# Decoder step: four page numbers in one load, and all value transfers of the sample attention issued by SyncE

## The chip, the core and the metric

The kernel runs on one core of a Trainium2 chip. A core has TensorE (PE in the profile), VectorE (DVE), ScalarE (ACT), GpSimd (POOL) and SyncE (SP), which only issues transfers and waits, and 16 DMA engines that move the data. SyncE and ScalarE each have a queue from which they issue transfers. The metric is the time of one execution in microseconds on the device.

## The reference

One layer of a hybrid decoder for a prompt of 512 rows and for 8 sample sequences of 8 new rows each (width 1024). The change concerns the attention of the samples. Each sequence b has two units, one for each mixer:

```python
# mixer A (m = 0): 8 heads x 64, window of 2048 cached keys, three dilated patterns
kk = jnp.concatenate([cache_win_k[b], k], 1);  vv = jnp.concatenate([cache_win_v[b], v], 1)
o = dilated_mix(q, kk, vv, L + jnp.arange(DS))
...
# mixer B (m = 1): 4 heads x 2 maps of 64, values of 128, over 16 pages of 128 rows
pk = ck[page_table].reshape(DB, P, N_HEADS_B, 2, HEAD_DIM)
pv = cv[page_table].reshape(DB, P, N_HEADS_B, 2 * HEAD_DIM)
a = softmax(q1 k1) - lam * softmax(q2 k2);  o = a @ v
```

Which pages belong to a sequence stands in `page_table` (8 x 16 whole numbers), an input. So the kernel has to read a page's number on the chip before it can issue the page's transfer. A page of keys or of values is 128 rows of 2 KB, 256 KB.

## The kernel before

**Stages.** Conditioning and input projection (to about 240 us), the prompt's attention (mixer A, to about 305), the sample attention together with the rest of the prompt's attention (mixer B), from about 310 to 655 us, then the output projection, the first norm, the gated ConvFFN and the second norm.

**Units and groups.** The list `sa` holds 16 units w = (m, b), mixers in turn. A unit's keys and values are cut in groups: m = 0 has three (two of 1 MB, one of 512 KB), m = 1 has four of four pages. Groups are numbered through, G = 0 to 55. Keys have 3 buffers (`kraw`), values 4 (`vg`).

**Work on a group.** VectorE transposes the keys (`turn_keys`, line 1145) and counts `kg_t`. TensorE scores them (`score_group`, line 1697). When all groups of a unit and its new rows are scored (`sa_s`), VectorE finds the minimum (lines 1243 to 1260), ScalarE takes exponentials (877 to 882), TensorE transposes them, and `weigh_group` (1729) multiplies with the values and counts `sa_vg`. The weighting of unit w's group g is placed behind the scoring of unit w+1's group g. Between these each unit also carries two units of the prompt's mixer B (`scores_b`, `turn_b`, `weigh_b`; ScalarE's `probs_b` at line 857 and `copy_b` at 866).

**Order on SyncE.** In one written-out order: for each G the keys of G, after `kg_t` says that buffer G-3 has been turned, then the values of group G-3 (`values_behind`, line 567), after `sa_vg` says that the buffer of four groups before is free; at the end of each unit from the third on the new rows of that unit (`load_new`, lines 425 and 426). Behind the last keys (G = 55) come the values of 52 to 55.

**Order on ScalarE.** `values_by_act` names the value groups that SyncE leaves out and ScalarE issues: of each unit but the first the groups 0 and 1 for m = 1, and group 1 for m = 0. They stand in ScalarE's order behind the copy at line 891, some ahead of `probs_b`, some behind (lines 892 to 898). ScalarE's activations behind them in its order wait for them to be issued.

**A page.** For a page of keys (lines 591 and 593) or values (446 and 448) the queue runs a load of the number from `pages` into a register (TENSOR_LOAD), a computation of bounds (FUSED_REGOPS), an assertion (SEQ_ASSERT), an address computation and the issue (DMA_DIRECT2D). Window loads have fixed addresses: keys 584 and 587, values 438 and 442.

Of the kernel before, what the change touches and what calls it, by code (L numbers as in the profile page):

```python
# [23 lines left out]
N_PAGES = PAST // PAGE  # L24
# [50 lines left out]
def build(nc, a, o, spill):  # L75
# [6 lines left out]
    with ctx:  # L82
        def sb(name, shape, dt=F32):
            return ctx.enter_context(nc.sbuf_tensor(name, shape, dt))
# [36 lines left out]
        pages = sb("pages", [1, DB * N_PAGES], I32)  # L121
# [250 lines left out]
        sa = [(m, b) for b in range(DB) for m in range(2)]  # L372
# [13 lines left out]
        for r, n in enumerate(rope_units):  # L386
            sec, t = units[n]
# [29 lines left out]

        def values_by_act(w, g):

            return w < len(sa) and w > 0 and (g < 2 if sa[w][0] else g == 1)  # L420

        def load_new(eng, w):

            m, b = sa[w]
            eng.dma_start(kn[0:DS, w % 2, :], k_s[DS * b:DS * b + DS, m, :]).then_inc(new_in[w % 2], 16)
            eng.dma_start(vn[0:DS, w % 2, :], v_s[DS * b:DS * b + DS, m, :]).then_inc(new_in[w % 2], 16)

        def load_values(eng, w, g):

            m, b = sa[w]  # L430
            win_v = flat_v[0][b].rearrange("(g r) h d -> g r (h d)", r=16)
            G = NG[w] + g
            vs = G % NV
            if G >= NV:
                eng.wait_ge(sa_vg, G - NV + 1)
            if m == 0 and g < 2:
                for t in range(4):
                    eng.dma_start(vg[vs][t:P:4, :, :],
                                  win_v[:, 4 * g + t, :].rearrange("(i m) f -> m i f", i=4)).then_inc(vg_in[vs], 16)
            elif m == 0:  # L440
                for t in range(2):
                    eng.dma_start(vg[vs][32 * t:32 * t + 32, :, :],
                                  win_v[96:128, 8 + 4 * t:12 + 4 * t, :]).then_inc(vg_in[vs], 32)
            else:
                for t in range(4):
                    pg = eng.value_load(pages[0:1, N_PAGES * b + 4 * g + t:N_PAGES * b + 4 * g + t + 1],
                                        min_val=0, max_val=a["cache_v"].shape[1] - 1)
                    eng.dma_start(vg[vs][t:P:4, :, :],  # L448
                                  flat_v[1][bass.ds(pg, 1)].rearrange("a (i m) h d -> m (a i) (h d)", i=4))\
                        .then_inc(vg_in[vs], 16)  # L450
# [3 lines left out]
        def _(sp):  # L454
# [105 lines left out]

            sp.wait_ge(page_in, 16)
            load_values(sp, 0, 0)
            load_values(sp, 0, 1)
            sp.wait_ge(w_used, CHUNK_AT[("ada", 9)] + 1)
            group_list = [(w, g) for w, (m, b) in enumerate(sa) for g in range(len(groups[m]))]

            def values_behind(G):

                if G >= 2 and not values_by_act(*group_list[G]):
                    if G == 2:  # L570
                        sp.wait_ge(pa_min, NU)
                    load_values(sp, *group_list[G])

            for w, (m, b) in enumerate(sa):
                win_k = flat_k[0][b].rearrange("(g r) h d -> g r (h d)", r=16)
                for g, nt in enumerate(groups[m]):
                    G = NG[w] + g
                    ks = G % NK
                    if G == 2:
                        sp.wait_ge(w_used, CHUNK_AT[("ada", 11)] + 1)  # L580
                    if G >= NK:
                        sp.wait_ge(kg_t, G - NK + 1)
                    if m == 0 and g < 2:
                        sp.dma_start(kraw[ks][:, :, :], win_k[:, 4 * g:4 * g + 4, :]).then_inc(kg_in[ks], 64)
                    elif m == 0:
                        for i in range(4):
                            sp.dma_start(kraw[ks][32 * i:32 * i + 32, 0:2, :],
                                         win_k[96:128, 8 + i:16:4, :]).then_inc(kg_in[ks], 16)
                    else:
                        for t in range(4):  # L590
                            pg = sp.value_load(pages[0:1, N_PAGES * b + 4 * g + t:N_PAGES * b + 4 * g + t + 1],  # L591
                                               min_val=0, max_val=a["cache_k"].shape[1] - 1)
                            sp.dma_start(kraw[ks][:, t, :], flat_k[1][bass.ds(pg, 1)].rearrange("a p h d -> (a p) (h d)"))\  # L593
                                .then_inc(kg_in[ks], 16)
                    if G >= 3:
                        values_behind(G - 3)
                if w >= 2:
                    sp.wait_ge(kn_t, w - 1)
                    sp.wait_ge(sa_pv, w - 1)
                    load_new(sp, w)  # L600
# [65 lines left out]
        def _(pool):  # L666
# [21 lines left out]
            for _, what, r in sorted(jobs):  # L688
                if what == "split":
                    n = CHUNK_AT[("in", r)]  # L690
                    for k in range(0, KT_D, 2):
                        if r == 0:
                            pool.wait_ge(in0_high, k // 2 + 1)
                        else:
                            pool.wait_ge(win_high, 4 * (r - 1) + k // 2 + 1)
                        w = slot(SLOT_OF[n])[:, k, :]
                        high, rest = pair_of(n, k)
                        nc.gpsimd.tensor_tensor(rest, w, high.bitcast(F32), ALU.subtract).then_inc(win_pool, 1)
                    if r == 0:
                        rest_of_ht(0)  # L700
                    continue
                s, t = units[rope_units[r]]
                sample_k = s in (1, 4) and t == TP
                pool.wait_ge(pj_d, r + 1)
                if not sample_k and r >= 4:
                    if (prev := last_t[r]) is not None:
                        pool.wait_ge(qk_t, prev)
                    if (q := last_store[r]) > 0:
                        pool.wait_ge(stg[r % 4], 16 * q)
                rows = P if t < TP else NS  # L710
                dst = k_s[:, s // 3, :] if sample_k else stage[0:rows, r % 4, :]
                nc.gpsimd.tensor_tensor(dst, tmp_a[0:rows, r % 2, :], tmp_b[0:rows, r % 2, :], ALU.add)\
                    .then_inc(rope_ok, 1)
# [56 lines left out]
        def _(act):  # L770
# [47 lines left out]
            for _, what, n in sorted(jobs):  # L818
                s, t = units[n]
                rows = P if t < TP else NS  # L820
                if what == "v":
                    act.wait_ge(pj_mm, n + 1)
                    dst = vp[:, t, s // 3, :] if t < TP else v_s[:, s // 3, :]
                    nc.scalar.activation(dst, bk(n % 4)[0:rows, :], ACT.Copy).then_inc(pj_a, 1)
                else:
                    k = tr_units.index(n)
                    act.wait_ge(qk_t, k + 1)
                    src = bk(4 + k % 2).rearrange("p (f t) -> p f t", f=4)
                    m0 = 8 * (s // 3)
                    for h in range(2):  # L830
                        last = nc.scalar.activation(qtp[64 * h:64 * h + 64, m0 + h:m0 + 8:2, P * t:P * t + P],
                                                    src[64 * h:64 * h + 64], ACT.Copy)
                    last.then_inc(qk_a, 1)
# [11 lines left out]
            act.wait_ge(out_sem, 16 * (TP * 2 + 2 * DB + 2))  # L845
            act.wait_ge(new_zero, 3)
            load_new(act, 0)
            load_new(act, 1)

            def probs_b(y):  # L850
# [17 lines left out]
            for w, (m, b) in enumerate(sa):  # L868
# [23 lines left out]
                if values_by_act(w + 1, 0):  # L892
                    load_values(act, w + 1, 0)
                probs_b(2 * w)
                if values_by_act(w + 1, 1):
                    load_values(act, w + 1, 1)
# [85 lines left out]
        def _(dve):  # L982
# [117 lines left out]
            jobs += [(5 * c - 1.4, "split", c) for c in range(1, 6)]  # L1100
            dve.wait_ge(rope_in, 16)
            for _, what, n in sorted(jobs):
                if what == "split":
                    for k in range(KT_D):
# [937 lines left out]
```

## Time and profile before

| what | value |
|---|---|
| median of 3 runs | 1250.76 us (1249.6 to 1254.75) |
| the profiled execution | 1249.29 us, its span 1247.3 us |
| PE busy | 1059.1 us, 85% of the span |
| DVE busy | 838.5 us, 67% |
| ACT busy | 269.2 us, 22% |
| POOL busy | 356.9 us, 29% |
| DMA | 276.55 MB, mean 222 GB/s |
| granted TensorE clock, mean | 0.911 |

A row of the stretches gives, for a stretch A:B in microseconds from the span's start, its length, then the busy time of PE, PEld (weight loads), DVE, ACT and POOL with the number of instructions in brackets, then the granted TensorE clock as a share, the DMA engines' busy share and GB/s. A row of the chain or of the timeline begins with its start and its length. Names with a q (SPq, ACTq) are the instructions of an engine's queue, issues of transfers above all. A merged row such as "x4" reaches from the start of its first instruction to the end of its last. A row on one line of the kernel gives the count and the least, median and greatest duration in nanoseconds.

### The profile page before, as it was taken

To read this page: it belongs to the slowest core of one execution; us is meant where nothing else is said; L and a number is where in the kernel's file an instruction comes from. 1 tells how busy PE (TensorE), PEld (TensorE's weight loads), DVE (VectorE), ACT (ScalarE), POOL (GpSimd) and SP (SyncE) were. 2 spreads that over 40 slices of the span, in tenths; PEclk is the share of its full clock that TensorE was granted. 3 is DMA by queue.
4 is the path that set the end of the run, shared out by engine and by line. 5 is a ranking of instruction groups with operands and counts; after the bars stand their busy time and mean duration, and the time that the engine had idled before them with its cause. 6 is when DMAs were issued, how large, how long until landed. Compare 5 with 4: busy or idle time off the path is not lost.

```text
span 1247.3 us, 24201 instructions
## 1 busy us (share of the span) xinstructions
PE 1059.1 (85%) x9389; PEld 856.2 (69%) x9389; DVE 838.5 (67%) x1521; ACT 269.2 (22%) x588; POOL 356.9 (29%) x378
## 2 busy tenths in 40 slices
PE   4599999999677677777776996999999999999994
PEld 2377777666455455555545774999999999777772
DVE  1657457267665767667749568367677676998968
ACT  0310010232222223222234103223222232100002
POOL 2333243100000000000007004356565565434323
PEclk8699999999787788779787897999999999999997
DMA  8948894686999999999991206177557731412202
GB/s 305 404 163 314 306 363 148 215 298 231 315 296 307 336 352 303 342 326 320 317 316 60 63 26 219 62 275 270 203 202 254 283 137 69 147 56 89 75 27 76
DMA packets 112551, 276.55 MB, mean 222 GB/s; under 512 B 9608, under 2 KB 33174, under 8 KB 108837
## 3 DMA queue, kind: packets, MB, share of 16 engines
q1 hardware_dynamic: 99125, 250.82, 59.2%
q10 hardware_dynamic: 13312, 24.19, 5.7%
q8 instruction: 75, 1.23, 0.4%
q14 instruction: 39, 0.32, 0.1%
HBM read 264.60 MB, written 76.69 MB: 274 GB/s over the span
## 4 chain that ended last, share of the span: by engine, by line
PE 58%; DVE 17%; SPq 10%; DMA 7%; issue 5%; POOL 2%; ACT 1%; ACTq 0%; DVEq 0%; POOLq 0%; PEldq 0%
PE wide L1572 16%; PE wide L1573 15%; PE wide L1574 15%; DVE ring L1145 3%; DMA ring<-in_cache_k 3%; SPq L591 3%; PE wide L1646 2%; SPq L593 2%; DMA ring<-in_w_ada 2%; PE wide L1635 2%; DVE ring_r L1077 2%; PE wide L1521 1%; SPq L448 1%; DMA ring<-in_w_down 1%; PE wide L1697 1%
## 5 line engine op out<-in xcount | busy, mean ns | idle before, releaser
L741 POOL TENSOR_TENSOR ring_r<-ring,ring_r 128x1024 fp32r<-128x1024 f32 x70 | 184.4, 2642 | 273.5 <-DVE ring_r L1037 204.5
L1572 PE MATMUL wide<-x_sb_r,ring_r 128*128 128x288 f32 x704 | 211.6, 301 | 8.2 <-DVE ht_r L1059 5.1
L1573 PE MATMUL wide<-ht_r,ring_r 128*128 128x288 f32 x704 | 209.4, 298 | 0.0
L1574 PE MATMUL wide<-x_sb_r,ring_r 128*128 128x288 f32 x704 | 208.6, 296 | 0.0
L1574 PE MATMUL wide<-ring_r,ht_r 128*128 128x512 f32 (+1 forms) x400 | 158.7, 397 | 0.0
L1145 DVE STREAM_TRANSPOSE ring<-ring 128x512 f32<-128x512 f32 x208 | 129.2, 674 | 34.7 <-DMA ring<-in_cache_k 34.7
L1572 PEld LDWEIGHTS wide<-x_sb_r,ring_r 128*128 128x128 f32 x704 | 133.4, 190 | 11.7 <-issue 11.2
L1574 PEld LDWEIGHTS wide<-x_sb_r,ring_r 128*128 128x128 f32 x704 | 134.2, 191 | 0.0
L1573 PEld LDWEIGHTS wide<-ht_r,ring_r 128*128 128x128 f32 x704 | 133.8, 190 | 0.0
L1697 PE MATMUL wide<-ring,x_sb 128*32 128x128 f32 (+1 forms) x1792 | 70.9, 309 | 49.5 <-DVE ring L1145 47.9
L1572 PE MATMUL wide<-ring_r,x_sb_r 128*128 128x512 f32 (+1 forms) x240 | 97.7, 407 | 11.0 <-DVE ht_r L1059 8.9
L1697 PEld LDWEIGHTS wide<-ring,x_sb 128*32 128x32 f32 x1792 | 54.5, 127 | 66.9 <-DVE ring L1145 57.5
L723 POOL COPY x_sb<-ring 32x128 f32<-32x128 f32 x64 | 18.4, 287 | 272.9 <-PE wide L1697 270.8
L1573 PE MATMUL wide<-ring_r,x_sb_r 128*128 128x512 f32 (+1 forms) x240 | 95.1, 396 | 0.0
L1572 PE MATMUL wide<-ring_r,ht_r 128*128 128x512 f32 (+1 forms) x220 | 88.2, 401 | 4.3 <-DVE ht_r L1397 2.4
L1574 PEld LDWEIGHTS wide<-ring_r,ht_r 128*128 128x128 f32 (+1 forms) x400 | 72.6, 181 | 21.5
L1573 PE MATMUL wide<-ring_r,ht_r 128*128 128x512 f32 (+1 forms) x220 | 86.7, 394 | 0.0
L1411 DVE SCALAR_TENSOR_TENSOR room<-room,vec_t 128x512 f32<-128x512 f32 x44 | 59.9, 1361 | 39.7 <-ACT room L954 39.6
L946 ACT ACTIVATE room<-wide,vec_t 128x576 f32<-128x576 f32 x44 | 32.7, 744 | 206.2 <-PE wide L1574 201.5
L1413 DVE SCALAR_TENSOR_TENSOR room<-room,vec_t 128x512 f32<-128x512 f32 x44 | 69.5, 1579 | 1.6
L1646 PE MATMUL wide<-room 128*128 128x128 f32 x320 | 58.3, 320 | 11.0 <-ACT room L866 9.8
L1037 DVE CAST ring_r<-ring 128x1024 fp32r<-128x1024 f32 x62 | 41.9, 687 | 36.1 <-DMA ring<-in_w_up 29.7
(225 smaller groups left out, 1894.0 us busy)
## 6 DMA issues: line engine op xcount, KB each, us to landing
ring<-in_cache_k SPq DMA_DIRECT2D x128, 256.0 KB
out_wks<-in_cache_win_k SPq DMA_DIRECT2D x8, 4080.0 KB, 19.0
out_wvs<-in_cache_win_v SPq DMA_DIRECT2D x8, 4080.0 KB, 24.7
ring<-in_w_ada SPq DMA_DIRECT2D x12, 2048.0 KB, 10.2
ring<-in_w_up SPq DMA_DIRECT2D x22, 1024.0 KB, 7.3
ring<-in_cache_win_k SPq DMA_DIRECT2D x16, 1024.0 KB
ring<-in_w_in SPq DMA_DIRECT2D x6, 2048.0 KB, 18.5
room<-in_cache_v ACTq DMA_DIRECT2D x32, 256.0 KB
```

The source lines that it names most:

```text
L591: pg = sp.value_load(pages[0:1, N_PAGES * b + 4 * g + t:N_PAGES * b + 4 * g + t + 1], min_val=0, max_val=a["cache_k"].shape[1] - 1)
L741: nc.gpsimd.tensor_tensor(rest, w, high.bitcast(F32), ALU.subtract).then_inc(wl_rest, 1)
L946: nc.scalar.activation(u_b[:, k % 2, 2:2 + NT].rearrange("p (h t) -> p h t", h=2), pair, ACT.Identity, bias=vec_t[:, 0, 48 + f:49 + f]).th ...
L1037: nc.vector.tensor_copy(pair_of(n, slice(k, k + 2))[0], slot(SLOT_OF[n])[:, k:k + 2, :]).then_inc(wl_high, 1)
L1145: last = nc.vector.transpose(ktg[:, G % NK, :, 32 * t:32 * t + 32], kraw[G % NK][:, t, :].rearrange("p (g d) -> p g d", d=32))
L1411: then(nc.vector.scalar_tensor_tensor(out=c_p, in0=u_b[:, k % 2, 1:1 + SEQ], scalar=tap(1), in1=c_p, op0=ALU.mult, op1=ALU.add))
L1413: nc.vector.scalar_tensor_tensor(out=c_p, in0=u_b[:, k % 2, 0:SEQ], scalar=tap(0), in1=c_p, op0=ALU.mult, op1=ALU.add)
L1572: nc.tensor.matmul(out, left[0], right[0], start=first, stop=False)
L1573: nc.tensor.matmul(out, left[0], right[1], start=False, stop=False)
L1574: return nc.tensor.matmul(out, left[1], right[0], start=False, stop=last)
L1646: last = nc.tensor.matmul(bank[:, 0:P], pt_b[:, u % 2, P * kb:P * kb + P], vp[:, kb, m, P * (n // 2):P * (n // 2) + P], start=(kb == 0), s ...
L1697: last = nc.tensor.matmul(bank[32 * nn:32 * nn + 32, at:at + nk], qbd[:, w % 2, g].rearrange("p i q -> p (i q)"), keys[:, g, 0:nk], start= ...
```

## The change

One instruction sequence reads the four page numbers of a group, for keys and for values, where four sequences read one each. And no value group is left to ScalarE: `values_by_act` is never true, so SyncE's `values_behind` issues every value group, at its place three groups behind the keys. Buffers, counts and waits are as they were.

```diff
         def values_by_act(w, g):
 
-            return w < len(sa) and w > 0 and (g < 2 if sa[w][0] else g == 1)
+            return False
...
+        def page_numbers(eng, b, g):
+
+            at = N_PAGES * b + 4 * g
+            _, numbers = nc.values_load_multi_w_load_instructions(pages[0:1, at:at + 4], engines=[eng.engine],
+                                                                  min_val=0, max_val=a["cache_k"].shape[1] - 1)
+            return numbers
...
-                for t in range(4):
-                    pg = eng.value_load(pages[0:1, N_PAGES * b + 4 * g + t:N_PAGES * b + 4 * g + t + 1],
-                                        min_val=0, max_val=a["cache_v"].shape[1] - 1)
+                for t, pg in enumerate(page_numbers(eng, b, g)):
                     eng.dma_start(vg[vs][t:P:4, :, :],
...
-                        for t in range(4):
-                            pg = sp.value_load(pages[0:1, N_PAGES * b + 4 * g + t:N_PAGES * b + 4 * g + t + 1],
-                                               min_val=0, max_val=a["cache_k"].shape[1] - 1)
+                        for t, pg in enumerate(page_numbers(sp, b, g)):
                             sp.dma_start(kraw[ks][:, t, :], flat_k[1][bass.ds(pg, 1)].rearrange("a p h d -> (a p) (h d)"))\
```

## Rows read from the trace of the kernel before

**Rows 1.** The page, busy time of TensorE over the span.

```profile
PE 1059.1 (85%) x9389; PEld 856.2 (69%) x9389; DVE 838.5 (67%) x1521; ACT 269.2 (22%) x588; POOL 356.9 (29%) x378
```

**Rows 2.** Busy time by stretches, the middle of the sample attention.

```profile
350.00:640.00 290.00, 207.55 (x3985) 150.72 (x3984) 191.22 (x501) 75.10 (x249) 13.77 (x48) 0.82 1.00 323
```

**Rows 3.** The chain of waits from 310 to 640 us: shares by line, two landings.

```profile
by line: issue 13.3%; DMA ring<-in_cache_k 11.7%; DVE ring L1145 11.4%; SPq L591 9.5%; SPq L593 7.7%; SPq L448 5.0%; PE wide L1697 4.7%; PE wide L1646 3.7%; SPq L446 3.5%; SPq L438 3.4%; PE wide L1751 2.5%; PE wide L1729 2.3%; ACT ht L877 1
...
413.16 6.31 DMA ring<-in_cache_k
...
537.82 9.21 DMA ring<-in_cache_k
```

**Rows 4.** The same chain, read from 499 to 541 us: where SyncE's queue begins.

```profile
499.56 0.37 SPq L584
```

**Rows 5.** SyncE's semaphore waits from 310 to 640 us, first and last of six.

```profile
SPq L584 <- DVE ring L1145: 4.9, 7, 1.7
...
SPq L438 <- PE wide L1729: 0.7, 1, 0.7
```

**Rows 6.** The timeline of SyncE's issues from 440 to 485 us.

```profile
441.25 8.26 SPq L593 DMA_DIRECT2D ring<-in_cache_k  x8
449.55 0.91 SPq L442 DMA_DIRECT2D room<-in_cache_win_v  x2
451.49 3.70 SPq L593 DMA_DIRECT2D ring<-in_cache_k  x4
455.29 0.78 SPq L425 DMA_DIRECT2D room<-ring  x1
...
456.88 1.07 SPq L584 DMA_DIRECT2D ring<-in_cache_win_k  x2
...
463.99 2.21 SPq L587 DMA_DIRECT2D ring<-in_cache_win_k  x4
467.00 4.72 SPq L448 DMA_DIRECT2D room<-in_cache_v  x4
...
478.50 2.69 SPq L438 DMA_DIRECT2D x_sb<-in_cache_win_v  x4
```

**Rows 7.** Busy time of a stretch in which SyncE issues eight key pages.

```profile
441.00:449.50 8.50, 5.50 (x91) 3.54 (x91) 6.76 (x22) 4.12 (x17) 1.15 (x4) 0.92 1.03 375
```

**Rows 8.** The timeline of all engines from 620 to 665 us, the stage's end.

```profile
620.07 3.71 SPq L593 DMA_DIRECT2D ring<-in_cache_k  x4
...
626.72 10.76 SPq L448 DMA_DIRECT2D room<-in_cache_v  x8
...
650.22 1.07 PE L1729 MATMUL wide<-room,ht 128*16 128x128 f32 x32
```

**Rows 9.** Queue instructions of lines 591, 593, 448, 438 and 584, each by itself.

```profile
L591 SPq TENSOR_LOAD <-pages x128: 262/269/867, 307.7 to 622.7; - x128
L591 SPq FUSED_REGOPS  x128: 152/152/188, 308.2 to 623.0; - x128
L591 SPq SEQ_ASSERT  x128: 18/18/37, 308.5 to 623.2; - x128
...
L593 SPq DMA_DIRECT2D ring<-in_cache_k x128: 333/338/1013, 308.7 to 623.4; - x128
...
L448 ACTq DMA_DIRECT2D room<-in_cache_v x32: 609/610/827, 325.3 to 589.1; - x32
...
L438 SPq DMA_DIRECT2D room<-in_cache_win_v x16: 599/656/1798, 350.7 to 565.9; - x16
L438 ACTq DMA_DIRECT2D room<-in_cache_win_v x16: 623/646/1382, 396.9 to 610.3; - x16
...
L584 SPq DMA_DIRECT2D ring<-in_cache_win_k x16: 365/450/712, 288.4 to 585.7; - x16
```

**Rows 10.** The timeline of ScalarE from 449 to 463 us.

```profile
450.91 4.63 ACTq L448 DMA_DIRECT2D x_sb<-in_cache_v  x4
455.64 0.61 ACT L857 ACTIVATE room<-room,mn 128x384 f32<-128x384 f32 x1 [4.89 <-DVE mn L1200]
```

**Rows 11.** VectorE's wait for cache keys, of the waits from 310 to 650 us.

```profile
DVE ring L1145 <- DMA ring<-in_cache_k: 34.7, 11, 6.9
```

## The prediction

> **What bounds the kernel now.** I read the page's table of engines first, then the stretches of the sample attention, then the chain of waits through it, then SyncE's own issues and waits, and at last ScalarE beside them. TensorE is the busiest engine of the whole span [rows 1], but the change touches only the sample attention, from about 310 to 640 us. In its middle TensorE is busy for 207.6 of 290 us and VectorE for 191.2, while the DMA engines are busy for all of it and move 323 GB/s [rows 2]. So the reader looks at loading there, and asks whether the transfers or their issue set the pace. The chain answers: in it lines 591, 593, 446, 448 and 438, where SyncE reads page numbers and issues loads, make up 29% of this stretch, the wait for cache keys to land 12%, and the keys' transposes 11% [rows 3]. From 499.56 us the chain is SyncE's queue without a break, line after line, up to a landing of 9.21 us that begins at 537.82 [rows 3, 4].
>
> SyncE hardly ever waits for a semaphore: the rows of its waits between 310 and 640 us are six and come to 14.9 us, 1.0 of them for the late weights [rows 5]. Its own work fills the rest. Eight key pages take 8.26 us from the first issue to the end of the last, four take 3.70: a step of (3.70 - 0.34)/3 = 1.12 us each, where 256 KB at 375 GB/s, the rate of a stretch in which SyncE issues eight key pages and nothing else, take 0.70 [rows 6, 7]. A value page takes (4.72 - 0.60)/3 = 1.37 us [rows 6].
>
> **SyncE's load now.** The last group of cache keys is issued from 620.07 to 623.78 us [rows 8]; that is the end I count to, about 314 us after 310. Ahead of it SyncE issues some 128 key pages (1.10 to 1.12 us each, about 141), 56 value pages (77), 28 window values at 0.67 (19), 16 short window values at 0.48 (8), 14 large window keys at 0.5 (7), 28 small ones at 0.47 (13), and 14 pairs of new rows (22, from 0.78 for the first of two that are alike) [rows 6]. That sums to about 287 us. The remaining 27 to 30 us are the 14 us of semaphore waits and some 15 us in which an issue takes longer than its usual time (a value issue goes up to 1798 ns where the median is 656) [rows 5, 9].
>
> **The change, part by part.** (a) One load in place of four. A page costs a load of 269 ns, a bound computation of 152 and an assertion of 18, then two short register steps (66 together) and 338 for the issue [rows 9]; the six leave gaps of about 45 ns each in the 1.12 us step. Three loads fewer save 3 x (269 + 45) = 0.94 us a group, if the load of four costs what a load of one does. I leave the checks at one per page. A group of keys then takes 4.48 - 0.94 = 3.54 us, one of values 5.48 - 0.94 = 4.54. Over 32 key groups this saves 30.1 us; over the 14 value groups that SyncE already issues ahead of the last keys, 13.2.
>
> (b) What comes onto SyncE. ScalarE issues 64 cache value pages and 16 + 12 window pages (of each kind the rows show one buffer) [rows 9]. Two of its 16 cache groups are those behind the last keys; 14 move ahead of them: 14 x 4.54 = 63.6 us. All 28 window issues move too, at (2.69/4 =) 0.67 us [rows 6]: 18.8. Sum for SyncE ahead of the last keys: 63.6 + 18.8 - 30.1 - 13.2 = +39 us.
>
> (c) How much of it is hidden. SyncE has about 29 us in which it isn't working, so if all of them fill up the end moves by 39 - 29 = +10 us; if none does, by 39. The 14 us of waits are mostly for a key buffer that VectorE has yet to turn [rows 5]; a SyncE that comes later finds it turned, and I take 11 of them back. Of the 15 us of slow issues I take 6, since transfers will be somewhat less crowded. That leaves 39 - 17 = +22 us.
>
> (d) What leaves ScalarE. A group's issues hold it for 4.63 us, and an activation of the prompt unit stands behind them [rows 10]. But these activations are off the chain here: the gap before line 857 is put to VectorE's mn, and no ScalarE queue time has a share in the chain's list [rows 3, 10]. I count 0; were each of 30 issuing blocks to cost TensorE half a microsecond, it would be 15 us gained, and only while SyncE leaves room.
>
> (e) The end. Behind the last keys SyncE will have four value groups and the new rows, 4 x 4.54 + 1.5 = 19.7 us, where now two groups end at 637.48. From 623.78 that ends at 643.5, plus some 4 us to land 647.5, in time for the last weighting, which starts at 650.22 [rows 8]. So the end hides it, with under 3 us to spare. The new semaphore waits of the moved values (for line 1729's group four earlier) now stand in front of the next keys on SyncE, and VectorE's transpose waits for those. By the order of the code such a group is weighted soon after the keys that SyncE has just sent for are turned; I put 0 to 2 us a pair of units, inside the waits that I kept.
>
> (f) Bounds of what the trace doesn't show. A load of four words is at least the 269 ns of one and at most four of them, 1.08 us; over 60 groups ahead of the last keys that is 0 to +49 us. I take the lower end, as it is the same instruction with the same round trip. Issues that stand closer together may cost more: a key page at 338 ns after 0.7 us of other work, the window keys of line 584 at 450 in direct succession, so at most 0.11 x 128 = +14 us [rows 9]. I take 0, since an address step stays between two issues. If the four checks shared one computation and one assertion, 3 x (152 + 18 + 90) = 0.78 us a group would go, -47 us over 60 groups, and SyncE would be no fuller than now; I leave them apart, as each number has its own bound.
>
> A page figure on this load, which the sum doesn't use: the Trainium skill (Runtime: NRT & Kernel Launch, Instruction fetch mechanics) says that such a load costs about 200 ns per register even in bulk. An estimate by it is 0.8 us for four, +0.53 us a group, +32 us, so 1305 instead of 1273. The row of 269 ns for one register neither supports nor excludes that.
>
> **The rivals.** Load priced by the word (slower still): the load of four takes about 0.87 us, 60 x 0.6 = +36 us on top, near 1309. For it: nothing in the trace has more than one word.
>
> No change: the DMA engines set the pace, busy all the time [rows 2], and who issues doesn't matter, so 1251. Against it: the step of 1.12 us is longer than the 0.70 of the transfer, and SyncE has less idle time than it is given work. The Trainium skill (DMA: Bandwidth & Descriptors, Issuing engines are not separate DMA queues) says that issuing from several engines saves only the sequencer's time, usually small beside the transfer. By that rule the change costs about nothing; here the trace disagrees on the size, 1.12 us of issuing to 0.70 of moving.
>
> Faster: the keys' landings. The chain's waits for cache keys are 11.7% of 330 us, 38.6, in five pieces of 6.31 to 9.21 us [rows 3]. ScalarE's queue puts value pages beside them; in the one queue they come behind the keys. If each of the five shrinks by 4 us, and SyncE's idle 29 us are all filled, the sum is +10 - 20 = -10, or 1241; shared checks, +39 - 47 = -8, come to about the same. It decides once the landings shrink by more than 2 us each. Against it: the same bytes go through the same engines, and a queue run by the slower issuer is what they would wait for instead.
>
> **How the numbers follow.** The profiled execution took 1249.29 us, the median of three is 1250.76; I add to the median: 1250.8 + 22 = 1273. Likeliest case (0.50): SyncE is the bound, 1260 to 1290, that is +10 to +39. Load by the word or closer issues costing more (0.18): 1290 to 1315. No change (0.17): 1245 to 1257. Faster (0.15): 1230 to 1244. The range 1248 to 1308 leaves out the faster case and a corner of the slowest, about 0.2. With half a per cent, 6.3 us, as what a measurement can tell, the slower cases hold 0.68, the same 0.17, faster 0.15.
>
> **What would show it.** In the profile of after: no ScalarE issue of a value transfer; SyncE's issues without pauses from 310 us to the last keys; load instructions on SyncE at 64 rather than 192, and their mean duration (0.27 or near 0.9 us) decides the first rival; the number of bound computations decides the shared-check case. VectorE's wait for cache keys (34.7 us now, [rows 11]) should rise by some 20 us, SyncE's semaphore waits fall, and GB/s of the stretch fall from 323 to about 300. Should the wait for keys fall and the stretch stay at 330 us, the DMA engines were the bound and I am wrong in (c).

## The result and the profile after

The changed kernel took 1291.1 us (median of 4 runs, 1286.5 to 1291.7) against 1250.2 us of the kernel before: a ratio of 1.0318, 95% interval 1.0294 to 1.0342, or +40 us (+37 to +43). It is slower, as forecast; the forecast was 1273 in a range of 1248 to 1308. The profiled execution took 1291.04 us, its span 1288.9.

The lines of the kernel have moved by three to seven: 593 is 596, 448 is 453, 438 is 445, 1145 is 1148. The loads of page numbers, 591 and 446 before, are both line 431 now, in the shared `page_numbers`.

Busy time by stretches. First one row of the kernel before, its sample attention with the tail; then the kernel after: the prompt part, the sample attention with its tail, the rest, and the stretch that answers to [rows 2].

```profile
308.00:656.00 348.00, 247.78 (x4698) 181.16 (x4697) 228.20 (x601) 91.39 (x297) 16.06 (x56) 0.81 0.99 319
```

```profile
0.00:308.00 308.00, 272.43 (x1427) 195.01 (x1427) 170.17 (x381) 47.68 (x110) 79.10 (x65) 0.96 0.79 277
308.00:697.00 389.00, 257.72 (x4688) 184.90 (x4687) 230.10 (x599) 92.25 (x297) 16.08 (x56) 0.79 0.88 281
697.00:1289.00 592.00, 538.61 (x3277) 478.60 (x3276) 441.49 (x544) 130.20 (x181) 262.65 (x257) 0.95 0.39 139
...
350.00:640.00 290.00, 190.94 (x3524) 136.36 (x3520) 174.35 (x453) 68.25 (x222) 13.78 (x48) 0.79 0.90 285
```

The first and third stretch are as long as before; what was 348 us (308 to 656, the same two edges of the work) is 389. All of the loss is in the sample attention. VectorE and ScalarE have the same work in it. The granted clock of TensorE is 0.79 there and was 0.81; a slower TensorE could hold up SyncE's queue only through a wait, and all of SyncE's waits come to 4.6 us (below). In the middle of the stretch, 350 to 640 us, the DMA engines went from a full share to 0.90, and from 323 to 285 GB/s, where about 300 were forecast: now they idle in part.

SyncE's semaphore waits from 310 to 690 us in the kernel after, which answer to [rows 5]; then VectorE's waits for landings from 310 to 650 us, to [rows 11].

```profile
SPq L431 <- DVE ring L1148: 2.2, 1, 2.2
SPq L445 <- PE wide L1732: 1.3, 2, 0.7
SPq L592 <- DVE ring L1148: 0.6, 1, 0.6
SPq L589 <- DVE ring L1148: 0.5, 1, 0.5
```

```profile
DVE ring L1148 <- DMA ring<-in_cache_k: 41.0, 15, 5.0
DVE ring L1148 <- DMA ring<-in_cache_win_k: 23.7, 14, 3.8
```

SyncE waits for 4.6 us in 380; its waits have all but gone. VectorE's wait for cache keys rose from 34.7 to 41.0 us in the same stretch, which is less than the 20 us more that were forecast; with the window keys, for which it had no such wait before, it waits 64.7.

The chain of waits, kernel after, 310 to 680 us, answers to [rows 3].

```profile
by line: SPq L453 17.3%; issue 15.2%; SPq L431 14.7%; SPq L596 12.0%; SPq L445 9.3%; DMA ring<-in_cache_k 5.2%; DMA ring<-in_cache_win_k 3.9%; SPq L592 3.4%; DVE ring L1148 3.4%; PE wide L1700 2.4%; SPq L425 1.9%; SPq L589 1.9%; SPq L449 1.
```

Lines 591, 593, 446, 448 and 438 had 29% of this chain; their successors 453, 431, 596 and 445 have 53%. The landings of cache keys fell from 12% to 5%, and window keys, which had no landing in the chain before, have 4%. Between 440 and 500 us nothing but SyncE's queue and its issue time is in it:

```profile
by line: SPq L453 22.9%; SPq L431 19.6%; issue 17.7%; SPq L596 13.8%; SPq L445 8.3%; SPq L592 6.4%; SPq L425 3.9%; SPq L426 3.5%; SPq L449 2.5%; SPq L589 1.8%; SPq L602 0.1%
```

The queue instructions one by one, kernel after, answer to [rows 9].

```profile
L431 SPq FUSED_REGOPS  x256: 147/150/185, 307.7 to 681.1; - x128
L431 SPq SEQ_ASSERT  x256: 18/18/37, 308.0 to 681.3; - x128
L431 SPq TENSOR_LOAD <-pages x64: 294/344/1006, 307.2 to 680.0; - x64
...
L453 SPq DMA_DIRECT2D room<-in_cache_v x64: 602/603/1575, 328.0 to 683.9; - x64
...
L596 SPq DMA_DIRECT2D ring<-in_cache_k x128: 332/333/1343, 309.0 to 663.6; - x128
```

The load of four numbers takes at least 294 ns where the load of one took 262. The bound computation and assertion are there 256 times, one for each page. At the median the issue of a key page is no slower at 0.54 us distance than at 1.1; the longest of them went from 1013 to 1343 ns.

SyncE's timeline near the end, kernel after, answers to [rows 8]; and the last weighting.

```profile
661.97 1.96 SPq L596 DMA_DIRECT2D ring<-in_cache_k  x4
665.49 3.05 SPq L453 DMA_DIRECT2D x_sb<-in_cache_v  x4
...
672.28 3.14 SPq L453 DMA_DIRECT2D x_sb<-in_cache_v  x4
676.99 7.48 SPq L453 DMA_DIRECT2D room<-in_cache_v  x8
```

```profile
691.04 1.07 PE L1732 MATMUL wide<-room,ht 128*16 128x128 f32 x32
```

The last keys are issued by 663.93 us, where it was 623.78: 40.15 us later. From there the last weighting starts 27.1 us on, where it was 26.4. So the 40 us arise ahead of the last keys.

### The profile page after: what moved, and what is told of

Read it like the earlier page. It is cut to its first block, busy times and chain, and to the rows that moved or that the text cites. A ratio compares the mean times of both kernels' runs of the same rounds, so it can differ in the third digit from the quotient of the medians.

```text
span 1288.9 us, 24007 instructions
## 1 busy us (share of the span) xinstructions
PE 1068.8 (83%) x9389; PEld 858.5 (67%) x9389; DVE 841.8 (65%) x1521; ACT 270.1 (21%) x588; POOL 357.8 (28%) x378
## 4 chain that ended last, share of the span: by engine, by line
PE 53%; SPq 19%; DVE 14%; DMA 6%; issue 6%; POOL 2%; ACT 0%; ACTq 0%; DVEq 0%; POOLq 0%; PEldq 0%
PE wide L1575 15%; PE wide L1577 14%; PE wide L1576 14%; SPq L453 5%; SPq L431 4%; SPq L596 3%; SPq L445 3%; DVE ring_r L1080 2%; PE wide L1649 2%; PE wide L1638 2%; PE wide L1524 2%; DMA ring<-in_w_ada 2%; DMA ring<-in_cache_k 1%; DMA ring<-in_w_down 1%; DVE ring L1148 1%
## 5 line engine op out<-in xcount | busy, mean ns | idle before, releaser
L1700 PE MATMUL wide<-ring,x_sb 128*32 128x128 f32 (+1 forms) x1792 | 76.8, 329 | 79.5 <-DVE ring L1148 79.1
L1700 PEld LDWEIGHTS wide<-ring,x_sb 128*32 128x32 f32 x1792 | 57.6, 137 | 101.3 <-DVE ring L1148 88.7
L726 POOL COPY x_sb<-ring 32x128 f32<-32x128 f32 x64 | 18.4, 287 | 306.5 <-PE wide L1700 284.1
L1575 PEld LDWEIGHTS wide<-ring_r,x_sb_r 128*128 128x128 f32 (+1 forms) x240 | 43.5, 181 | 27.7 <-issue 13.0
```

Of the source, the lines that this page charges most:

```text
L1575: nc.tensor.matmul(out, left[0], right[0], start=first, stop=False)
L1700: last = nc.tensor.matmul(bank[32 * nn:32 * nn + 32, at:at + nk], qbd[:, w % 2, g].rearrange("p i q -> p (i q)"), keys[:, g, 0:nk], start= ...
```

## The experiments

### SyncE's queue made lighter or heavier in single parts

Two theories. Q: SyncE's issuing sets the pace, and what is added or taken on its queue ahead of the last keys moves the end one for one, down to the next bound. The rivals: D, the DMA engines are the bound; S, it isn't the cost of issuing but that one queue, not two, carries the transfers.

**The load of four alone** (e1): the changed kernel, in which ScalarE keeps its groups.

```diff
-            return False
+            return w < len(sa) and w > 0 and (g < 2 if sa[w][0] else g == 1)
```

> One part of the change alone: four page numbers in one load, while ScalarE keeps the value groups that it had. SyncE's work ahead of the last keys falls by 60 - 14 = 46 groups x 0.94 = 43 us. Theory Q (SyncE's issuing sets the pace, and its time ahead of the last keys counts in full): the time falls well below 1250, until the DMA engines, now busy for the whole stretch at 323 GB/s, become the bound; at their 375 GB/s the stretch of 330 us could shrink to about 285, so 1215 to 1235. Rival D (the DMA engines were the bound before): 1245 to 1251. Rival S (one queue moves data more slowly than two, and that alone made the change slow): about 1250.

Measured: 1240.7 us, ratio to before 0.9923 (0.9895 to 0.9950). Faster, but by 10 us and not by 15 to 35. The waits of SyncE in this kernel, 310 to 640 us, and its chain's list from 310 to 620:

```profile
SPq L431 <- DVE ring L1148: 22.5, 13, 3.6
SPq L589 <- DVE ring L1148: 11.3, 7, 2.3
SPq L592 <- DVE ring L1148: 4.7, 5, 1.6
SPq L445 <- PE wide L1732: 4.1, 4, 1.7
SPq L431 <- PE wide L1732: 1.0, 1, 1.0
```

```profile
by line: DMA ring<-in_cache_k 19.4%; DVE ring L1148 16.8%; issue 12.5%; PE wide L1700 8.1%; PE wide L1732 5.0%; PE wide L1649 4.3%; SPq L596 3.9%; PE wide L1754 3.6%; DVE maskt L1253 3.2%; SPq L431 3.0%; DVE ht L1249 2.5%; PE wide L1772 2.1
```

With 43 us less to do by the sum, SyncE waits 43.6 us for others where it was 14.9, mostly for turned key buffers, and its lines fall to some 4% each or less. The bound has moved: the kernel before stood only 10 us above another one. All three theories missed the figure; Q has the sign, with a floor nearer than I put it.

**The other part alone** (e2): the kernel before with `values_by_act` never true, and a load for each page.

```diff
-            return w < len(sa) and w > 0 and (g < 2 if sa[w][0] else g == 1)
+            return False
```

> The other part alone: SyncE issues all values, with one load for each page number as before. Ahead of the last keys SyncE gets 14 x 5.48 + 18.8 = 95.5 us more work. Theory Q: 1335 to 1346. With 17 us taken back from SyncE's waits, as in the prediction: 1329. Rival S (the single queue, whatever the issues cost): about 1291, as with the whole change.

Measured: 1347.6 us, ratio 1.0775 (1.0747 to 1.0803), +97 us. The work added was 95.5 us by the sum. Q to within 2 us, though in part by luck, as the section on the prediction shows. S can't explain the size: queue and order are those of the changed kernel, which is 56 us faster (60 groups x 0.94 = 56). SyncE's one wait between 310 and 740 us in this kernel:

```profile
SPq L446 <- PE wide L1729: 0.2, 1, 0.2
```

**The changed kernel without the checks** (e3). The bound computations and assertions are left out; nothing that is computed changes.

```diff
-                                                                  min_val=0, max_val=a["cache_k"].shape[1] - 1)
+                                                                  min_val=0, max_val=a["cache_k"].shape[1] - 1,
+                                                                  skip_runtime_bounds_check_because="a page table names pages of the pool")
```

> The changed kernel, without the bound computation and the assertion on each page number (the result is the same, since every page number lies in the pool). About 0.25 us x 240 = 60 us leave SyncE's queue ahead of the last keys; everything stays in one queue. Theory Q: 1291 falls by up to 60, to 1235 to 1250, less if the DMA engines become the bound. Rival S (one queue is slow by itself): within 5 us of 1291.

Measured: 1240.2 us, ratio to before 0.9903 (0.9869 to 0.9937). All values in one queue, ScalarE issuing none, and 51 us below the changed kernel. S is out: one queue is as fast as two were. The time is that of e1, but the same bound isn't shown. SyncE waits only 14.8 us here (310 to 640 us), and its lines have a third of the chain from 310 to 620 us, much as in the kernel before. The stretch from 350 to 620 us, then the chain's list:

```profile
350.00:620.00 270.00, 196.32 (x3752) 142.84 (x3756) 184.46 (x485) 72.97 (x241) 13.77 (x48) 0.82 1.03 330
```

```profile
by line: DMA ring<-in_cache_k 13.0%; issue 12.0%; SPq L597 10.4%; SPq L454 9.4%; DVE ring L1149 8.6%; SPq L446 7.3%; PE wide L1701 4.6%; SPq L431 4.1%; PE wide L1733 3.3%; DMA ring<-in_cache_win_k 3.3%; PE wide L1755 2.3%; SPq L593 2.3%; DV
```

**Idle page numbers in the kernel before** (e4). Three numbers are read and checked and not used, in each cache value group of SyncE.

```diff
+                if eng is nc.sync:
+                    for t in range(3):
+                        eng.value_load(pages[0:1, N_PAGES * b + 4 * g + t:N_PAGES * b + 4 * g + t + 1],
+                                       min_val=0, max_val=a["cache_v"].shape[1] - 1)
```

> The kernel before, with three page numbers more read and checked, and not used, in each cache value group that SyncE issues: 3 x 0.56 = 1.7 us on SyncE, 14 times ahead of the last keys, 24 us, with no transfer moved. It asks how much new work SyncE can take before the end moves. The prediction's step (17 of 29 us are room): 1250 + 7 = 1257. Theory Q with no room at all: 1274. Rival D (DMA engines are the bound): 1251.

Measured: 1270.2 us, ratio 1.0147 (1.0118 to 1.0175), +18.4 us (+15 to +22) for 24 us of work. The last keys are issued by 642.99 in the timeline, 19.2 us later than before:

```profile
639.29 3.70 SPq L597 DMA_DIRECT2D ring<-in_cache_k  x4
```

SyncE's waits up to there fell from 13.9 to 8.4 us. So of these 24 us the kernel before took up 5, where the prediction had 17 of 39. D predicted no change and is out for the kernel before. No transfer was added or moved here, so this is the cleanest sign that SyncE's instructions set the pace.

### What the floor is, and how steep the slope above it

**Load of four and no checks, ScalarE keeps its groups** (e5): the edits of e1 and e3 together.

> Four numbers in one load, ScalarE keeps its groups, and no bound computation or assertion: SyncE's queue is lighter than in any other kernel here, by about 46 x 1.0 = 46 us against the one with the load alone (1241). Rival D2 (with that load alone the DMA engines, share 1.02 and 330 GB/s in the stretch, are already the bound): 1236 to 1243. Theory Q still (SyncE remains the bound there, by its waits for turned keys): 1215 to 1230.

Measured: 1242.8 us, ratio 0.9950 (0.9931 to 0.9969), no better than e1 or e3. SyncE now waits 99.5 us; the two largest rows of its waits, 310 to 640 us:

```profile
SPq L431 <- DVE ring L1149: 54.1, 17, 6.3
SPq L590 <- DVE ring L1149: 20.3, 8, 3.3
```

Between e1 and e5 SyncE's work no longer counts: that is the floor, at about 1240.

**The same with fewer bytes** (e6). A quarter of each value page isn't loaded; the weighting takes what lies in the buffer.

```diff
-                    eng.dma_start(vg[vs][t:P:4, :, :],
-                                  flat_v[1][bass.ds(pg, 1)].rearrange("a (i m) h d -> m (a i) (h d)", i=4))\
+                    eng.dma_start(vg[vs][t:P:4, 0:3, :],
+                                  flat_v[1][bass.ds(pg, 1)].rearrange("a (i m) h d -> m (a i) (h d)", i=4)[:, 0:3, :])\
```

> The same, and each value page loads 96 of its 128 rows (a quarter of the cache values stays out and old content is weighted in its place): 128 x 64 KB = 8.4 MB less of 110 MB, 25 us at 330 GB/s. D2 (the DMA engines are the floor): 1212 to 1222. Rival C (the floor is the round of transposes, scores and softmax, with the buffers): within 5 us of the kernel with the light queue.

Measured: 1237.7 us, ratio 0.9917 (0.9889 to 0.9945); its interval overlaps that of e5. 25 us of transfers less are worth about 5 by the medians. In the two profiled executions the last keys are issued 12 us earlier (604.99 against 616.93). So bytes still count for a part, a fifth to a half of their time, and the DMA engines alone are not the floor, though they are busy for all of the stretch, here too (350 to 600 us):

```profile
350.00:600.00 250.00, 181.10 (x3698) 134.29 (x3697) 176.72 (x469) 69.66 (x227) 13.84 (x48) 0.87 1.00 320
```

The chain in it is landings of keys 20.3% and their transposes 17.5%, and SyncE waits for turned buffers. This fits a round through the three key buffers (issue, landing, transpose, buffer free), but I made no run with other buffers, so what makes up the floor stays open.

**ScalarE issues one group in four** (e7).

```diff
-            return False
+            return w < len(sa) and w > 0 and sa[w][0] == 1 and g == 0
```

> The changed kernel, but ScalarE issues group 0 of each page unit: 7 groups of 4.54 us leave SyncE ahead of the last keys, 32 us, and the groups of the windows stay on SyncE. Theory Q (each us on SyncE counts until the floor of about 1240): 1291 - 32 = 1259. If the order of waits on SyncE rather than its work made the change slow, another figure: the semaphore waits there are only 5 us, so no more than 5 us off.

Measured: 1265.8 us, ratio to before 1.0127 (1.0104 to 1.0151). 25 us below the changed kernel, where 32 were taken from SyncE by the sum; its semaphore waits rose to 8.3 us. The figure missed by 7 us. Counted in the trace, SyncE had only 27 us less to do.

**Value pages issued in the form of key pages** (e8). The value rows lie in another order than the weighting takes them.

```diff
-                    eng.dma_start(vg[vs][t:P:4, :, :],
-                                  flat_v[1][bass.ds(pg, 1)].rearrange("a (i m) h d -> m (a i) (h d)", i=4))\
+                    eng.dma_start(vg[vs][:, t, :], flat_v[1][bass.ds(pg, 1)].rearrange("a p h d -> (a p) (h d)"))\
```

> The changed kernel, with each value page issued in the form of a key page (128 partitions, one row of 2 KB each; the rows lie elsewhere in the buffer than the weighting takes them, so the values are weighted in a wrong order). Bytes and number of rows are the same; an issue takes 0.34 us in place of 0.60. 112 issues ahead of the last keys: 29 us less on SyncE. Theory Q: 1291 - 29 = 1262. If the transfers rather than their issue were the bound: 1291.

Measured: 1257.2 us, ratio 1.0057 (1.0036 to 1.0079), 34 us below the changed kernel for the 30 us taken from SyncE by the sum. The same bytes in rows of the same 2 KB cost 333 ns to issue in place of 602:

```profile
L453 SPq DMA_DIRECT2D room<-in_cache_v x64: 332/333/822, 327.1 to 652.4; - x64
```

In one table: SyncE's work ahead of the last keys against the kernel before, from the predicted terms; the time in which SyncE doesn't wait for a semaphore, counted in the trace from 310 us to the end of the last key issue; and the time of the kernel. The last column is the ratio to executions of the kernel before that were taken together with that kernel's.

| kernel | work by the sum, us | not waiting, us | time, us | against before |
|---|---|---|---|---|
| e5, load of four, no checks | about -90 | 212 | 1242.8 | -0.5% |
| e1, load of four | -43 | 265 | 1240.7 | -0.8% |
| e3, changed, no checks | 39 - 60 = -21 | 292 | 1240.2 | -1.0% |
| before | 0 | 300 | 1250.2 | |
| e7, ScalarE keeps one group | 39 - 32 = +7 | 322 | 1265.8 | +1.3% |
| e8, key form | 39 - 30 = +9 | 324 | 1257.2 | +0.6% |
| e4, idle loads | +24 | 325 | 1270.2 | +1.5% |
| changed | +39 | 349 | 1291.1 | +3.2% |
| e2, values only | +96 | 406 | 1347.6 | +7.8% |

There is a floor at 1240, and above it the time grows by about 1 us for 1 us of the sum. Against the counted column it is less: 40 us of time for 49, 97 for 106, because the first of it goes into SyncE's waits. The kernel before stood 10 us above the floor. The best of them is e1 or e3; e1 keeps all checks and is 10 us faster than before and 50 faster than the change.

## Why the prediction was right in kind and short in size

**The mechanism (a and b) was right.** SyncE's queue got more to do than the shorter load saved, and the last keys are issued 40.15 us later for it. By category the trace gives, against the kernel before: key pages -30 us (30.1 forecast), window values +17 (18.8). The four-word load saves what was assumed, less 0.03 us a group. The checks stayed one per page. That SyncE's work is what counts is shown by e2 and e3 from both sides, and by e4 without moving a transfer.

**Step (c) failed: "I take 11 of them back ... Of the 15 us of slow issues I take 6".** The first half of it was right and the second wrong. SyncE's semaphore waits ahead of the last keys went from 13.9 to 4.6 us, so 9 us were taken back. But the time in which SyncE doesn't wait went from 300 to 349 us: 49 more, where the sum had 39 - 6 = 33. The end moved by 49 - 9 = 40. That this is nearly the 39 of (a) and (b) is luck, for it is two terms that cancel: the 9 us of waits, and 10 us of work that the sum doesn't have. e2 shows the same on a larger scale: 106 us more of not waiting, all 13.9 us of waits gone, the last keys 93 us later.

The mis-sized term is that of the slow steps, in two ways.

First, the slow steps were work. What I had summed to 287 us (with 14 pairs of new rows, where 13 lie ahead of the last keys) is 300 when counted. A page load right behind certain issues takes longer than 0.27 us, in both kernels and with nothing to wait for that the profile shows. In the chain of the kernel before, 499 to 541 us, the issue of new rows and the load behind it:

```profile
514.32 0.87 SPq L426
515.24 0.84 SPq L591
```

And in the chain of the kernel after, 440 to 500 us, the same pair, a load behind a large window transfer, and the slowest load:

```profile
447.44 0.70 SPq L426
448.20 0.81 SPq L431
...
476.42 0.45 SPq L589
476.93 0.53 SPq L431
...
496.00 1.01 SPq L431
```

I counted the excess over the median as idle.

Second, the moved groups brought more of it. The value pages take 139 us where they took 80: 59 more, and the forecast had 50. With all groups on SyncE there are 14 value loads right behind a large window transfer, where there were 6 (a seventh came after a wait). And some issues of pages come out late: a value issue reaches 1575 ns, where SyncE's took 724 at most. The value issues have 6.1 us above their median in all, and had 1.3. It isn't that the queue is full: in e5, whose SyncE waits 99.5 us, value issues reach 1331 ns, and in e2, which waits 0.2 us in all, 1041. The mean issue of a key page is 351 to 363 ns in the three kernels with a load for each page and 369 to 428 in the six with the load of four, where the issues of a group stand closer. So (f), which took the price of closer issues at 0, had the median right and missed a tail: against e2, 112 value issues at a mean of 657 ns in place of 625 and 126 key issues at 369 in place of 354, some 5 us. What makes these issues late stays open.

**Step (d), nothing from ScalarE, held.** e3 and e5 both have a light SyncE, one with all values and one with ScalarE's share: 1240.2 and 1242.8, with intervals that overlap. As SyncE is fuller in e3, that doesn't measure what a freed ScalarE is worth by itself; in the changed kernel SyncE's queue accounts for the loss, and a gain beside it doesn't show. The bound of 15 us in (d) counted 30 issuing blocks; there are 16 cache groups and 7 of windows, 23, so 11.5.

**Step (e), a hidden end, held.** It was to be 19.7 us of issues behind the last keys and is 20.5 (663.93 to 684.47); the last weighting moved by 0.7 us relative to the keys. By the semaphore events of the trace the last value page lands 3.4 us after its issue, for which the prediction had some 4, and 3.2 us before that weighting.

**The bounds (f).** The load of four costs 294 ns at least against 262: near the lower end, as taken. The rival priced by the word is out. The Trainium skill (Runtime: NRT & Kernel Launch, Instruction fetch mechanics) gives about 200 ns per register for this instruction. Its section Terms has it load from HBM, while here it reads SBUF, where three more registers cost about 30 ns. So the figure doesn't carry over, and the prediction applied it where the page doesn't. Closer issues cost nothing at the median, 333 ns against 338.

**The rivals.** "No change" is out: e4 and e2. It rested on a DMA share of 1.0, and that share held at 1250 us as well as at 1240, so it doesn't show a bound. The Trainium skill's rule (DMA: Bandwidth & Descriptors, Issuing engines are not separate DMA queues) has two halves. That a second issuing engine saves only time on the sequencer agrees, since e3 with one queue is as fast as e5 with two. That this time is usually small beside the transfer doesn't hold here: 0.70 us of moving, 1.12 to 1.37 of issuing, and 97 us lost in e2. The faster rival had the right observation, that key landings shrink in the chain (12% to 5%), and the wrong conclusion. The DMA share fell to 0.90, and what left the chain was taken by SyncE's lines.

With nothing taken back in (c) the sum is 1250.2 + 39 = 1289, within the measured 1287 to 1293, but only by that cancelling: 9 us of waits did go, and 10 us of work weren't in the sum.

## What to carry to other kernels

Write down, for the queue that issues, each instruction of its step against the bytes that it sets moving: where a step takes longer than its transfer, a second issuing engine can be worth nearly its whole time, and so can each register step that is cut, until another bound comes up. Here that was after 10 us. Idle time of a queue is what its waits for semaphores show and not the difference from a sum of medians; what exceeds the medians is work, and work that is moved brings its own. A queue that hardly waits has little room, whatever the DMA engines' share says. And a part of a change should be tried alone: here the load of four gained 10 us, and moving the transfers cost 50.

## What the runs showed of the hardware

- Reading four numbers from SBUF into registers takes 0.29 us at least and 0.34 at the median, one takes 0.26 and 0.27.
- An issue's cost depends on the form of the transfer, also at equal bytes: 256 KB take 333 ns as 128 partitions x one row and 602 ns as 32 partitions x 4 rows.
- Bound computation and assertion take 150 + 18 ns with gaps of 0.04 to 0.05 us: 0.25 us a page, and 51 us of a kernel whose queue is the bound (e3 against the change).
- A page load directly behind an issue of 16 KB of new rows takes 0.77 to 1.01 us (before, changed, e2). Where SyncE had paused for 0.6 and 1.4 us behind the same issue, it took 0.46 (before).
- An issue's cost has a tail: key pages at a median of 0.33 us reach 1.34 us in the changed kernel, with a mean of 0.37.
